# A two-layer hybrid trunk on one core: the K half of the rotary step leaves the shared stretch and a spare PSUM bank, the state-space split and the convolution segments move to earlier places

## The reference, cut to what matters

```
for l in range(2):
    h = rmsnorm(x, norm1_g[l]) * (1 + sc1) + sh1
    q, k, v, ca, cb, su, gates = split(h @ w_in[l])
    q, k = apply_partial_rope(q), apply_partial_rope(k)
    y_attn = sliding_window_attention(q, k, v, sinks) @ w_attn_o[l]
    y_conv = conformer_conv(ca, cb, 31 taps, depthwise, layernorm, silu) @ conv_pw_w[l]
    y_ssm = s5_ssm(su, complex diagonal state) through a GLU
    x = x + g1 * ((gate_a*y_attn + gate_c*y_conv + gate_s*y_ssm) @ w_out[l])
    h2 = rmsnorm(x, norm2_g[l]) * (1 + sc2) + sh2
    x = x + g2 * ((silu(f_gate) * f_up) @ w_ffn_out[l])
```

## Time and profile before

| | us |
|---|---|
| median of three runs | 979.15 (977.47 to 979.83) |
| the profiled execution | 977.47 |
| its span in the trace | 975.6 |

### The profile page before, as it was taken

The page is one execution under the profiler, slowest core; times in us unless marked ns, Lnnn a source line. Parts: engine busy times, 40 slices in busy tenths (PEclk is TensorE's granted clock), DMA queues, the critical chain, the costliest instruction groups (busy, mean ns, idle before and its releaser), DMA issues.

```text
span 975.6 us, 16235 instructions
## 1 busy us (share of the span) xinstructions
PE 926.7 (95%) x6917; PEld 783.7 (80%) x6917; DVE 669.4 (69%) x913; ACT 462.7 (47%) x540; POOL 9.4 (1%) x11
## 2 busy tenths in 40 slices
PE   5989999989999999999999999899999899999994
PEld 2888876667678888899989997567777799999994
DVE  4883999998567765473556758999947754444545
ACT  4684147624545565544445223574274544343432
POOL 2000000000000000000000000000000000000000
PEclk9999999999999999999999999899999999999998
DMA  8984356668696466566667334556869545555521
GB/s 356 237 266 138 112 187 215 216 183 306 268 283 216 153 224 223 199 210 230 209 173 210 120 106 173 179 190 192 297 228 331 180 173 195 174 189 199 173 87 43
DMA packets 128630, 196.13 MB, mean 201 GB/s; under 512 B 30793, under 2 KB 90705, under 8 KB 122415
## 3 DMA queue, kind: packets, MB, share of 16 engines
q1 hardware_dynamic: 128247, 195.03, 60.1%
q10 hardware_dynamic: 312, 0.08, 0.0%
HBM read 194.02 MB, written 1.06 MB: 200 GB/s over the span
## 4 chain that ended last, share of the span: by engine, by line
PE 53%; DVE 29%; ACT 7%; issue 5%; DMA 4%; SPq 2%; ACTq 0%; DVEq 0%
PE bank L569 15%; PE bank L570 15%; PE bank L571 15%; DVE wlo L1395 8%; DVE yc L1680 7%; DMA raw<-in_w_mod 3%; ACT whi L1062 3%; PE bank L607 2%; PE bank L665 2%; PE bank L832 1%; PE bank L689 1%; DVE blx L1653 1%; ACT h L1077 1%; DMA raw<-in_w_attn_o 1%; SPq L452 1%
## 5 line engine op out<-in xcount | busy, mean ns | idle before, releaser
L1395 DVE TENSOR_TENSOR wlo<-raw,whi 128x2048 fp32r<-128x2048 f32 (+1 forms) x135 | 302.8, 2243 | 219.6 <-PE bank L571 184.0
L1062 ACT ACTIVATE whi<-raw 128x2048 fp32r<-128x2048 f32 x132 | 252.2, 1911 | 111.7 <-PE bank L571 34.8
L569 PE MATMUL bank<-hhi,whi 128*128 128x256 f32 x928 | 265.6, 286 | 0.8 <-DVE wlo L1395 0.8
L570 PE MATMUL bank<-hlo,whi 128*128 128x256 f32 x928 | 262.6, 283 | 0.0
L571 PE MATMUL bank<-hhi,wlo 128*128 128x256 f32 x928 | 262.4, 283 | 0.0
L569 PEld LDWEIGHTS bank<-hhi,whi 128*128 128x128 f32 x928 | 177.8, 192 | 7.9 <-issue 5.0
L570 PEld LDWEIGHTS bank<-hlo,whi 128*128 128x128 f32 x928 | 177.9, 192 | 0.8 <-issue 0.2
L571 PEld LDWEIGHTS bank<-hhi,wlo 128*128 128x128 f32 x928 | 177.8, 192 | 0.0
L569 PE MATMUL bank<-whi,bhi 128*128 128x512 f32 x304 | 121.3, 399 | 1.9 <-DVE wlo L1395 1.9
L570 PE MATMUL bank<-wlo,bhi 128*128 128x512 f32 x304 | 118.8, 391 | 0.0
L571 PE MATMUL bank<-whi,blo 128*128 128x512 f32 x304 | 118.5, 390 | 0.0
(11 more groups left out here) (258 smaller groups left out, 885.6 us busy)
## 6 DMA issues: line engine op xcount, KB each, us to landing
raw<-in_w_mod SPq DMA_DIRECT2D x48, 1024.0 KB, 5.3
raw<-in_w_ffn_in SPq DMA_DIRECT2D x44, 1024.0 KB, 5.2
raw<-in_w_in SPq DMA_DIRECT2D x38, 1024.0 KB, 7.0
raw<-in_w_ffn_out SPq DMA_DIRECT2D x22, 1024.0 KB, 4.9
raw<-in_w_out SPq DMA_DIRECT2D x8, 1024.0 KB, 8.1
raw<-in_w_in SPq DMA_DIRECT2D x16, 256.0 KB, 4.5
raw<-in_ssm_glu_b SPq DMA_DIRECT2D x4, 1024.0 KB, 7.4
raw<-in_ssm_glu_a SPq DMA_DIRECT2D x4, 1024.0 KB, 6.1
```

The lines of the kernel that those rows point to most:

```text
L569: mm(o, w_hi, a_hi, start=start, stop=False, skip_group_check=True)
L570: mm(o, w_hi, a_lo, start=False, stop=False, skip_group_check=True)
L1062: fn(whi[mi % N_HI][:, :], raw[SLOT[item]][:, :], ACT.Copy).then_inc(s_hi, 1)
L1395: part = V.tensor_tensor(wlo[mi % N_LO][:, n], raw[SLOT[("main", *divmod(mi, NB))]][:, n], whi[mi % N_HI][:, n].bitcast(F32), ALU.subtract)
```

## The change

Four tables and one bank assignment change; no arithmetic does, and no instruction is added or dropped.

```diff
-SSM_SPLIT_AT = [z + 13 for z in Z_AT]
-
-ROPE_AT, V_TURN_AT = 17, 18
+SSM_SPLIT_AT = [z + 11 for z in Z_AT]
+
+ROPE_Q_AT, ROPE_K_AT = 17, 18
...
-CONV_AT = [{t0 + (43 - t0) * n // 15: divmod(n, 8) for n in range(16)} for t0 in (18, 15)]
+CONV_AT = [{t + 3 * n // 2: divmod(n, 8) for n in range(16)} for t in (18, 15)]
...
-B_SPREAD_AT = [{0: 0, 2: 1}, {PREP_AT + 3: 0, PREP_AT + 5: 1}]
+B_SPREAD_AT = [{0: 0, 1: 1}, {PREP_AT + 3: 0, PREP_AT + 5: 1}]
...
-                if (l, c) == (0, 2):
-                    pe.wait_ge(kf_ready, 1)
-                o = (b_s, b_t, b_y)[c]
+                if c == 2:
+                    pe.wait_ge(rope_ready, 3 * l + 1)
+                o = (b_s, b_t, b_s)[c]
...
-                pe.wait_ge(rope_ready, 3 * l + 2)
+                if l == 0:
+                    pe.wait_ge(kf_ready, 1)
                 for c, t0 in enumerate((0, CHUNK, P)):
-                    last = nc.tensor.transpose(b_t[:, c * P:(c + 1) * P], vT[:, t0:t0 + P], ident[:, :])
+                    last = nc.tensor.transpose(b_y[:, c * P:(c + 1) * P], vT[:, t0:t0 + P], ident[:, :])
...
-                if t == ROPE_AT:
-                    for c in range(3):
-                        rotate(l, c)
-                if t == V_TURN_AT:
+                if t == ROPE_Q_AT:
+                    rotate(l, 0)
+                    rotate(l, 1)
+                if t == ROPE_K_AT:
+                    rotate(l, 2)
                     v_transposes(l)
```

More of the change, by code:

```diff
@@ L1591, in rope @@
                 w = 2 if c < 2 else 1
-                src = halves((b_s, b_t, b_y)[c][:, :])[:, 0:w, :]
+                src = halves((b_s, b_t, b_s)[c][:, :])[:, 0:w, :]
                 q = qT[:, 2 * c:2 * c + 2, :] if c < 2 else kT[:, :].rearrange("p (o t) -> p o t", o=1)
@@ L1600, in v_copy @@
                 dve.wait_ge(vt_ready, l + 1)
-                V.tensor_copy(vv[:, :, :], b_t[:, 0:3 * P].rearrange("p (c d) -> p c d", c=3)).then_inc(v_ready, 1)
+                V.tensor_copy(vv[:, :, :], b_y[:, 0:3 * P].rearrange("p (c d) -> p c d", c=3)).then_inc(v_ready, 1)
             def softmax_max(l, r):
@@ L1804, in side @@
                     taps_in(0)
-                if t == ROPE_AT:
-                    for c in range(3):
-                        rope(l, c)
-                if t == V_TURN_AT:
+                if t == ROPE_Q_AT:
+                    rope(l, 0)
+                    rope(l, 1)
+                if t == ROPE_K_AT:
+                    rope(l, 2)
                     v_copy(l)
```

## The result

| | before | after |
|---|---|---|
| median | 978.43 us (977.47 to 979.83, four runs) | 987.32 us (986.64 to 991.41, four runs) |
| profiled execution | 977.47 us | 986.26 us |
| its span | 975.6 us | 984.4 us |

The changed kernel is slower by a ratio of 1.0087, with a 95% interval of 1.0066 to 1.0107: +8.5 us (6.5 to 10.5). Forecast was slower, +5.8 us, with a range up to 989.5; the sign and the range held, the size was a third too small.

The account below looks back on a forecast made before the run. VectorE's list was taken as the path in layer 0 until TensorE's last low-weight wait, then TensorE's. Start 0.3, layer 0 5.2 and layer 1 0.3 sum to +5.8 us: 985.0 us on the median, range 980.8 to 989.5.

Parts of the forecast that it names:

- the rule of segments ahead of a block's low weights: Both layers: block i's low weights stand behind all segments with t up to 2i - 3, at 3.17 or 2.37 us each.
- the walk along VectorE's list: Layer 0: counting segments and idle times on VectorE puts block 20's low weights at 216.7 us instead of 208.61.
- Start: Layer 0 preparation rounds: the moved spread of B lengthens TensorE's first wait by about 1.9 us and removes the second: +0.3.
- third rival: Both layers: TensorE's clock falls behind new stalls of about 3 us; up to +5, 990 us; chance 0.10.
- its own first step: Preparation rounds of layer 0: the second spread of B, moved earlier, makes one longer TensorE wait of two; +0.3 us.
- Layer 0: Block 20 starts 6.7 us late and block 21 5.2 us late, both for low weights: +5.2 us, bounds +3.6 and +6.5.
- the first of the two corrections: Layer 0, block 22: its weights, loaded once block 20's low weights are done, could come late: up to +0.8 us.
- The second correction: Layer 0, 265.17 us: TensorE's wait of 1.20 us for a modulation load could absorb as much of the delay.
- Layer 1: Vanished VectorE idle times put TensorE some 3.7 us ahead, but block 20's low weights take it all back: +0.3 us.
- the wait for K: Scores of round 0 wait for k, about +1 us in layer 0, to about 602.6 in layer 1; neither reaches the end.
- TensorE made nothing up: First rival, layer 0 behind block 20: TensorE has headroom and makes up the delay; -3.4, 975.8 us; chance 0.05.
- The new wait was paid in full: Second rival, layer 0: ScalarE's high part adds no VectorE idle time and the tail absorbs; +1.8, 981.0 us; chance 0.15.

Follow-up runs that it names:

- e1: Kernel before with only the new places of the convolution segments: 987.95 us against 978.59, ratio 1.0098.
- e5: Changed kernel with the convolution segments back at their old places: 979.33 us against 977.67 for the kernel before, ratio 1.0016.
- e2: Kernel before with only the second spread of B moved to follow block 1: 979.95 us against 978.59, ratio 1.0012.
- e11: Kernel before with one layer 0 segment moved from t = 38 to t = 37: 979.71 us against 978.20, ratio 1.0016.
- e4: Kernel before with only K's rotary step and the V transposes' bank as in the changed kernel: 977.39 us against 978.59, ratio 0.9990.
- e12: Kernel before with layer 1's split one place earlier and layer 0's segments respaced, 11 ahead of block 20's low weights: 969.15 us against 978.27, ratio 0.9914.
- e6: Changed kernel with K's rotary step and the V transposes back at their old places: 988.40 us against 977.67 for the kernel before, ratio 1.0105.

## Why the prediction was right, and where its size was off

**What bounds the kernel, and the rule of segments ahead of a block's low weights: right.** VectorE's list sets layer 0. Block 20's low weights were done at 218.56, against 208.61 before: 2.0 us of that came from the start and 8.0 from layer 0, where the walk along VectorE's list had +8.1. Block 20 was 6.7 us late in layer 0 by itself (8.65 less 1.97), forecast 6.7. Block 21 was 5.0 late (7.02 less 1.97), forecast 5.2. VectorE's idle time ahead of the split was 3.64, forecast 3.6; the stall for the norm of round 1 was 2.86, forecast 3. The half clock behind it (159.7 to 163.1) was covered as assumed: at block 16 layer 0's delay is 4.6 us (182.29 before, 188.83 after, less 1.97), less than the 6.7 that low weights impose at block 20. e1 and e5 show by both routes that the segments are the loss.

**Start: the term was mis-sized, +0.3 forecast, +1.9 over four profiles (1.2 in medians).** The waits were as forecast, one of 3.36 instead of 1.58 and 1.42. What the step left out is the clock, as far as the profiles tell: 6.8 us at half clock in the changed kernel, beginning inside that wait, and e2's table shows that the loss goes with it. The prediction's third rival spoke of new stalls of 3 us in the layers and overlooked that its own first step made one of 3.4 us.

**Layer 0: +5.2 forecast, +6.1 measured. The step that failed is the first of the two corrections.** It saw that a later load could be late for block 22 and took the load of the weights (up to +0.8). These landed 7.1 us after their issue instead of the 9.1 of before, and their low part was done at 229.93, ahead of TensorE. What was late was the modulation load, which stands behind them in SyncE's list, and it cost 2.3 (232.17, and e11 by itself). The prediction moved the pair of loads by 8.1 and TensorE by 5.2; less the 0.35 us that the modulation load had in hand before (222.52 to 222.87), that makes a wait of 2.5. The second correction came as described: the wait of 1.20 at 265.17 is gone at 273.24, and with it 1.2 us of the delay. 5.0 + 2.3 - 1.2 is 6.1.

**Layer 1: +0.3 forecast, +0.7 measured, and right for partly wrong reasons.** The scores came at 610.61, which is 602.5 without the 8.1 us of layer 0 (forecast 602.6), and no half clock stands behind the norm. But the forecast priced the wait for K at nothing and let TensorE arrive at the norm with its clock up and 3.7 us to the good. In fact the clock fell at the scores, inside a wait of 3.90, TensorE reached the probabilities at 624.07, 1.3 us later than before instead of 1 us waiting, and its lead at block 12 was 1.8 us. It made no difference to the end, because block 20's low weights came when the walk had them (693.06 against 685.1 + 8.1) and took back whatever lead there was: +0.3 at block 20, as forecast. The other 0.4 is the modulation load of block 22 again (1.09 us at 705.38) less a wait of 0.7 that went at block 28.

**The rivals.** TensorE made nothing up: from block 23 to block 27 of layer 0 it stays at +9.3 to within 0.02 us, although it has no wait there. The Trainium skill (Perfetto Trace Analysis, Identifying the Most-Contended Engine) names the busy share of TensorE's weight loads as one of two measures of its headroom. This trace speaks against reading it that way here: they are busy 99.9 of 142 us in layer 0's stretch (second line of the windows above), and yet nothing was made up. The new wait was paid in full. The clock did fall in new places, three of them, and the part of that rival that came true is the start's. In layer 1 it was hidden, and e4 shows that a stretch moved ahead of the stall can even be a gain. The rival was to be decided by the length of the stall, with nothing shown between 1.58 and 4.47 us. The kernel before does have a case in between, outside the stretches that were read: TensorE waits 1.68 us at 34.34, and its clock is at half from 35.15 to 38.56, while e12 waits 1.85 us at 34.28 and keeps its clock.

**The parts do not add.** Alone they give +9.6, +1.2, -3.9 and -1.0, which is +5.9, against +8.5 together. By the table of block starts the parts sum to +3.5 in layer 0, where the whole has +6.1, and to about -0.4 in layer 1, where it has +0.7. In layer 0, e1's segment at t = 22 had filled an idle time of 1.66 us; in the whole the split stands ahead of it and makes that idle time one of 3.64 that nothing fills. That is about 1.7 of the 2.6; the rest was not followed up. In layer 1 the split alone gives 4.9 us and next to the moved segments only 3.2 (e6 against e1, +3.5 and +6.7), since the low weights of block 20 then limit what is kept.

## What to carry to other kernels

Where one engine's in-order list feeds another, count the work ahead of each item that the other waits for, block by block: that walk was right here to 0.2 us in layer 0 wherever the idle times along it were counted too (e1's expectation missed one of 1.66). Then do the same for the loads that these items release. A load that stands behind others in the list lands when they are through, so it is their release that has to be early, not only its own (2.5 us here for one segment moved by one place, e11). And test the parts of a bundled change alone: of four, one made all of the loss, and one alone was worth 3.9 us. In layer 1 only, one place later, and together with the opposite of the bad one in layer 0, it was worth 7.9.
